# Position bias of the second block: factors of the product exchanged, results laid by query through DRAM

## The reference, cut to what matters

```python
bias = rel_bias[t5_bucket_2(pos_sel - pos_b[..., None])]   # 32 buckets, 16 heads
logits = jnp.einsum('bqhc,bqkc->bhqk', q_b, kv_sel) * scale
logits = logits + jnp.transpose(bias, (0, 3, 1, 2))
```

## Time and profile before

| | before |
|---|---|
| median of 3 runs | 1357.74 us (1356.25 to 1359.26) |
| profiled execution, its own time | 1356.31 us |
| span of that execution, first to last instruction | 1354.5 us |
| PE busy / PEld busy | 1335.7 us (99%) / 1194.7 us (88%) |
| DVE busy | 937.5 us (69%) |
| ACT busy | 419.5 us (31%) |
| POOL busy | 171.9 us (13%) |
| mean granted TensorE clock | 0.999 |

### The profile page before, as it was taken

The page is one execution under the profiler, slowest core; times in us unless marked ns, Lnnn a source line. Parts: engine busy times, 40 slices in busy tenths (PEclk is TensorE's granted clock), DMA queues, the critical chain, the costliest instruction groups (busy, mean ns, idle before and its releaser), DMA issues.

```text
span 1354.5 us, 21285 instructions
## 1 busy us (share of the span) xinstructions
PE 1335.7 (99%) x8873; PEld 1194.7 (88%) x8873; DVE 937.5 (69%) x1492; ACT 419.5 (31%) x892; POOL 171.9 (13%) x147
## 2 busy tenths in 40 slices
PE   9999999999999999999999999999999999999997
PEld 7976899988898599988888788889999995999986
DVE  4885798657598488867662778776887854856653
ACT  2154333220226333322056304435742103100101
POOL 3300322030200033114020000003100100011100
PEclk9999999999999999999999999999999999999999
DMA  9532567576432257756623251217644544545440
GB/s 321 187 124 94 187 222 276 213 274 215 169 126 93 94 208 281 258 210 225 216 63 105 85 184 63 79 62 255 209 144 142 217 161 151 162 151 187 171 171 31
DMA packets 127808, 229.76 MB, mean 170 GB/s; under 512 B 7094, under 2 KB 33998, under 8 KB 127458
## 3 DMA queue, kind: packets, MB, share of 16 engines
q1 hardware_dynamic: 123354, 218.26, 46.9%
q0 software_dynamic: 3952, 9.95, 2.2%
q10 hardware_dynamic: 407, 0.20, 0.1%
HBM read 227.30 MB, written 2.15 MB: 169 GB/s over the span
## 4 chain that ended last, share of the span: by engine, by line
PE 87%; DVE 7%; DMA 3%; issue 1%; ACT 1%; SPq 0%; DVEq 0%
PE acc L2033 55%; PE scr L2033 16%; PE pvw L2033 9%; DVE mid L1457 2%; DMA ring<-in_w_up 1%; PE scr L2132 1%; PE ptb L2141 1%; DMA ring<-in_w_in 1%; PE pvw L2631 1%; PE scr L2624 1%; DMA hid<-in_x 1%; DVE ring L1279 1%; PE scr L2602 1%; PE ptb L2033 1%; DVE ring L1219 1%
## 5 line engine op out<-in xcount | busy, mean ns | idle before, releaser
L2033 PE MATMUL acc<-y,ring 128*128 128x128 f32 (+2 forms) x1216 | 206.3, 325 | 1.1 <-ACT y L919 1.1
L2033 PEld LDWEIGHTS acc<-y,ring 128*128 128x128 f32 (+1 forms) x1216 | 182.9, 191 | 18.8 <-issue 2.9
L2033 PE MATMUL acc<-x,ring 128*128 128x128 f32 (+1 forms) x832 | 120.7, 299 | 0.0
L2033 PEld LDWEIGHTS acc<-x,ring 128*128 128x128 f32 x832 | 110.9, 192 | 5.8 <-issue 1.0
L2033 PE MATMUL acc<-ring,big 128*128 128x256 f32 (+1 forms) x376 | 115.5, 453 | 0.0
L2033 PEld LDWEIGHTS acc<-ring,big 128*128 128x128 f32 x376 | 70.6, 190 | 33.3 <-issue 26.9
L2033 PE MATMUL acc<-ring,hid 128*128 128x256 f32 (+1 forms) x364 | 98.8, 417 | 0.0
L860 ACT ACTIVATE ring<-ring,silc 128x512 f32<-128x512 f32 x96 | 60.1, 709 | 92.0 <-DMA ring<-in_ada_w 92.0
L2033 PEld LDWEIGHTS acc<-ring,hid 128*128 128x128 f32 x364 | 68.4, 190 | 21.7 <-issue 14.3
L2033 PE MATMUL acc<-ysq,ring 128*128 128x128 f32 x592 | 71.9, 275 | 0.1
L2033 PEld LDWEIGHTS acc<-ysq,ring 128*128 128x128 f32 x592 | 68.9, 192 | 0.4 <-ACT ysq L1008 0.4
(11 more groups left out here) (540 smaller groups left out, 2710.2 us busy)
## 6 DMA issues: line engine op xcount, KB each, us to landing
ring<-in_w_in SPq DMA_DIRECT2D x24, 2048.0 KB, 9.0
ring<-in_w_up SPq DMA_DIRECT2D x16, 2048.0 KB, 8.6
ring<-in_w_down SPq DMA_DIRECT2D x16, 2048.0 KB, 7.9
ring<-in_ada_w SPq DMA_DIRECT2D x12, 2048.0 KB, 12.9
ring<-in_w_ffn_in SPq DMA_DIRECT2D x22, 1024.0 KB, 6.7
ring<-in_w_out SPq DMA_DIRECT2D x6, 2048.0 KB, 8.1
ring<-in_w_o_ssd SPq DMA_DIRECT2D x4, 2048.0 KB, 8.1
ring<-in_w_ffn_out SPq DMA_DIRECT2D x4, 2048.0 KB, 7.6
```

Source lines behind the costliest of these rows:

```text
L2033: ins = pe.matmul(dst, w, m, start=start, stop=stop, is_transpose=turned, skip_group_check=True)
```

## The change

PE's two operands change places: the 64 columns of `blk` are now stationary, and 256 columns of the steps move. A matmul gives 64 rows (group and head) x 256 columns, and there are four for one bank: they go in turn to the lower and upper 64 partitions, two to each half of the bank (`bias_part`). A bank is one of 16 halves of chunks (`bias_made`), with group and head on the partitions and 4 positions x 256 on the free side. So that queries are what is spread over the chunks and keys are the 256 columns, the threshold's sign and the comparison are turned (`thr` is position plus `lo`, and `is_ge`). ACT and DVE copy a bank as it stands, 128 x 512.

`bias_made` lies in `hid` as `bias2` does. When both banks of a chunk are drained, POOL writes them to DRAM in two DMAs of 64 x 4 x 256 floats (256 KB; 16 such DMAs, 4.2 MB). When all have landed, four DMAs of 64 x 4096 floats (1 MB each) read them back into `bias2`, queries on the partitions. DVE waits for these four ahead of `logits2` at `b2 == FIRST2`.

```diff
--- before.py
+++ after.py
@@ -273,6 +273,7 @@
         isc, iwork = big[:, 12:14, :], big[:, 14:16, :]
         relu2 = work[:, 0:8, :].rearrange("p (a b) t -> p a b t", a=4)
         bias2 = hid[:, :, :].rearrange("p (t h) s -> p t h s", t=TT)
+        bias_made = hid[:, :, :].rearrange("p (n j) s -> p n j s", j=2)
         xtok2 = hid[:, 0:16, :].rearrange("p a b -> p (a b)").rearrange("p (t d) -> p t d", t=TT)
         ys = hid[:, 16:32, :]
         q2, qi2 = mid[:, 0:16, :], mid[:, 16:24, :]
@@ -305,6 +306,7 @@
         blank = upad[:, :, :].rearrange("p a b -> p (a b)")
         strips = nc.dram_tensor("strips", (4 * P * 2 * T + T,), F32).ap()
         acum_store = nc.dram_tensor("acum_store", (SSD_HEADS, T), F32).ap()
+        bias_store = nc.dram_tensor("bias_store", (64, 4 * HEADS2, T), F32).ap()
         gain_store = nc.dram_tensor("gain_store", (2, D), F32).ap()
         strip_rows = nc.dram_tensor("strip_rows", (4, 2 * T), F32).ap()
 
@@ -584,6 +586,16 @@
                 for c in range(DC):
                     pool.dma_start(gain_store[w:w + 1, c * P:(c + 1) * P].rearrange("o p -> p o"), mcol[:, 2 + w, c:c + 1]).then_inc(gains_out, 16)
 
+            for ci in range(8):
+                pool.wait_ge(drained, HEAD_ACCS + ACCS + DEPTH * LAYER_ACCS + BIAS_END[ci])
+                for i in range(2):
+                    pool.dma_start(bias_store[8 * ci + i:8 * ci + 8:2].rearrange("s p k -> p s k"),
+                                   hid[64 * i:64 * i + 64, 4 * ci:4 * ci + 4, :]).then_inc(bias_out, 16)
+            pool.wait_ge(bias_out, 16 * (5 + 16))
+            for g in range(4):
+                half = slice(64 * (g % 2), 64 * (g % 2) + 64)
+                pool.dma_start(bias2[half, g // 2, :, :], bias_store[:, HEADS2 * g:HEADS2 * g + HEADS2, :]).then_inc(bias_in, 16)
+
             def acum_row_pair(g, u):
 
                 if g >= 2:
@@ -907,10 +919,8 @@
 
             def bias_back(ci):
 
-                dst = bias2.rearrange("p t h (g s) -> p t s g h", g=4)
-                for t in range(TT):
-                    b = full()
-                    copied(dst[:, t, 8 * ci:8 * ci + 8], b[:, :, :].rearrange("p a b -> p (a b)").rearrange("p (s g h) -> p s g h", s=8, g=4))
+                for half in range(2):
+                    copied(bias_made[:, 2 * ci + half], full()[:, :, :])
 
             def modulated(first, gain, shift):
 
@@ -1333,7 +1343,7 @@
                 steps.mark(dve.tensor_copy(posqf[:, :], posq))
                 steps.mark(dve.tensor_copy(thr[:, :], posk[:, :]))
                 steps.sync()
-                steps.mark(ts(thr[:, :], thr[:, :], lo[:, 0:1], None, ALU.subtract))
+                steps.mark(ts(thr[:, :], thr[:, :], lo[:, 0:1], None, ALU.add))
                 steps.mark(ts(posq, posq, 6, None, ALU.arith_shift_right))
                 steps.mark(ts(post[:, :], post[:, :], 6, None, ALU.arith_shift_right))
                 steps.sync()
@@ -1392,7 +1402,7 @@
 
                     dve.wait_ge(filled, HEAD_ACCS + DEPTH * LAYER_ACCS + BIAS_END[ci - EARLY_BIAS])
                 tt(steps_of[ci % 3], over(posqf[:, :], 8), thr[:, 8 * ci:8 * ci + 8].unsqueeze(2).broadcast_to([P, 8, T]),
-                   ALU.is_le).then_inc(step_ready, 1)
+                   ALU.is_ge).then_inc(step_ready, 1)
 
             def head_combine(i, dst):
 
@@ -1412,8 +1422,7 @@
             def first_bias_back(t):
 
                 dve.wait_ge(filled, HEAD_ACCS + DEPTH * LAYER_ACCS + t + 1)
-                dve.tensor_copy(bias2.rearrange("p t h (g s) -> p t s g h", g=4)[:, t, 0:8],
-                                acc[t][:, :, :].rearrange("p a b -> p (a b)").rearrange("p (s g h) -> p s g h", s=8, g=4)).then_inc(drained, 1)
+                dve.tensor_copy(bias_made[:, t], acc[t][:, :, :]).then_inc(drained, 1)
 
             for l in range(DEPTH):
                 done = l * LAYER_ACCS + HEAD_ACCS + ACCS
@@ -1655,6 +1664,8 @@
                     conv2(b2 - 1)
                 if b2 in (0, 1):
                     select(b2)
+                if b2 == FIRST2:
+                    dve.wait_ge(bias_in, 16 * (8 + 4))
                 if b2 >= FIRST2:
                     for i in range(2):
                         k = 2 * (b2 - FIRST2) + i
@@ -2524,19 +2535,18 @@
                     ins = mm(ms, ones[:, which, :], src[:, c, :], c == 0, c == chunks - 1)
                 ins.then_inc(ms_full, 1)
 
-            def bias_part(b, ci, t, parts):
-
-                flat = b[:, :, :].rearrange("p a b -> p (a b)")
-                for s in parts:
-                    ins = mm(flat[:, 64 * s:64 * s + 64], steps_of[ci % 3][:, s, t * P:(t + 1) * P],
-                             blk[:, :, :].rearrange("p a b -> p (a b)"), True, True)
+            def bias_part(b, ci, half):
+
+                for s in range(4):
+                    ins = mm(b[64 * (s % 2):64 * (s % 2) + 64, s // 2, :], blk[:, :, :].rearrange("p a b -> p (a b)"),
+                             steps_of[ci % 3][:, 4 * half + s, :], True, True)
                 return ins
 
             def bias_products(ci, tiles=range(TT)):
 
                 pe.wait_ge(step_ready, ci + 1)
                 for t in tiles:
-                    bias_part(free_bank(), ci, t, range(8)).then_inc(filled, 1)
+                    bias_part(free_bank(), ci, t).then_inc(filled, 1)
 
             def turn(t, h, flat):
```

## The result

The changed kernel takes 1346.53 us (median of 5 runs, 1345.9 to 1348.08), the one before 1357.67 (5 runs): ratio 0.9924, 95% interval 0.9913 to 0.9935, that is 8.8 to 11.8 us less. The profiled execution took 1347.19 us, 9.12 less than that of before (1356.31); its span is 1345.2 us in place of 1354.5.

A forecast was written before the change was run, and what follows sets the result against it. TensorE, busy 99% of the span, was taken as the bound; 8.6 us from the second stretch plus 0.35 from the first, about 9.0, led to 1348.3 us, chance 0.70, range 1346.0 to 1352.2 (own range 1346.7 to 1350.2).

The forecast's parts named there:

- Where the gain lies: Bias products on TensorE: saving in the later gapless run moves everything behind it; earlier saving ends waiting for VectorE and ScalarE.
- second stretch: 160 bias records without a gap, 712.14 to 730.06 us; forecast 9.3 us in place of 17.9, 8.6 us less.
- B: Length of the second stretch, up to the transposes of `kvn`; forecast 8.6 us shorter.
- A: Length from the first bias product to the first product of the second stretch; forecast 0.35 us shorter.
- The price of a product: TensorE bias matmul, 64 stationary and 256 moving columns: taken as 0.116 us, one half's matmul running beside the other's.
- The other bound: TensorE bias matmul without overlap of the two halves: 0.223 us a record.
- Rival 1: Bias products' halves do not overlap: 0.223 us each, only 0.35 us gained, 1357 us, no change; chance 0.08.
- VectorE and ScalarE keep up: Compares and bank copies in the second stretch make TensorE wait for nothing: cost 0, with 0.3 us kept for copies.
- Rival 3: ScalarE's bank copies still cost 1.0 us and come late, some 2.3 us in all: 1350.6 us; chance 0.11.
- The first stretch: 96 bias records around the transposes from 683.91: 0.35 us gained by VectorE's shorter copy and ScalarE's earlier transposes, bounds 0 and 0.5.
- DRAM: Bias written out and read back by POOL, 8.4 MB: cost 0, reads ending about 785, 14 us before the logits.
- rival 2: Granted clock falls around the first stretch as TensorE idles: 3.6 us more, 1352 us; chance 0.07.

The follow-up runs named there:

- e2: Changed kernel with all bias products written to the lower 64 partitions, none to the upper; median 1355.78 us, ratio 1.0000 to the kernel before.
- e4: Changed kernel with ScalarE's 14 bank copies into a strided destination, as before the change; median 1347.49 us, ratio 0.9934 to the kernel before.
- e1: Changed kernel with products of three early banks done twice, 24 more records where TensorE waited; median 1346.40 us, ratio 0.9931 to the kernel before.
- e5: Kernel before the change with the changed kernel's plain bank copies on ScalarE and VectorE, products as they were; median 1355.39 us, ratio 0.9996.
- e9: Changed kernel with only VectorE's two copies of chunk 0 strided as before the change; one run, 1347.13 us.
- e8: Changed kernel with the four DRAM reads held on POOL until VectorE's convolution of the fifth double tile; median 1363.09 us, ratio 1.0051 to the kernel before.
- e7: Changed kernel with a fourth step buffer, chunk 3 compared and multiplied earlier, ahead of the gapless bias products; median 1344.91 us, ratio 0.9918 to the kernel before.
- e10: Changed kernel as it is, run again for a second look at the granted clock; one run, 1348.43 us.
- e3: Changed kernel with a chunk's eight matmuls four to the lower, then four to the upper partitions, except chunk 1; median 1348.89 us, ratio 0.9950 to the kernel before.

## Why the prediction was right

- **Where the gain lies.** Right: the second stretch moves the rest of the program, the first ends in a wait. B gave 9.12 us (forecast 8.6), A 0.58 (forecast 0.35), together 9.70, of which 9.36 show from the mark to the end. The sum was 8.95, the ratio's interval holds it. That the profiled executions as a whole also differ by 9.12 is chance.
- **The price of a product.** Right by the form that the trace already had the earlier trace rows: 0.116 taken, 0.119 by busy time, and 0.110 as 8.80 / 80, which is what B's extra 0.5 us come from. The other bound, 0.223, was measured in e2 (0.224). Rival 1 was priced rightly and is excluded.
- **VectorE and ScalarE keep up.** Right, with less room than counted for the compares: 0.12 us at chunk 7 where I had 0.5, as the products came sooner; and 0.18 us for the copies, where I had counted none at worst. Rival 3 is real if the stride is kept: 1.4 us in e4, where I had 2.3. Its price took the length of a lone strided copy, 1.04, for the pace of several in a row, which is 0.9.
- **The first stretch.** The size was too small and its reason half right. I had 0.35 us with an upper bound of 0.5; it is 0.67 where the clock holds (e1) and 0.58 in the profile of the changed kernel. I priced it by VectorE's copy and named the earlier transposes for ScalarE's part alone. The copy alone brings nothing (e5); the earlier transposes are 0.41 of 0.67 us, and the copy the rest (e9).
- **DRAM.** Right, and with 44 us to spare where I counted 14: the writes were done by 729.15 and not 743, the reads by 754.9 and not 785. That each us of lateness costs about one was shown by e8.
- **The clock.** Here the step failed that gave rival 2 a chance of 0.07. The argument was that the gaps are shorter than the 4 us at the end of the program; the clock fell with gaps of at most 2.13 us, in four of the six profiles with the changed first stretch. What was wrong on the other side is the price: 3.6 us were forecast, 0.1 to 1.4 came, because the low level lay mostly beside waits. That the result is the forecast's in spite of it is in part luck. By the Trainium skill ("TensorE: Matmul & The Clock Gate", Part 1) an idle array falls back to the lower level; here it fell though short runs of matmuls came between the waits, of which the longest was 2.13 us.
- The predicted 1348.3 lies 1.8 us above the median. The start was not the error: I had 1357.3, the median was 1357.67. The medians differ by 11.1 us and my sum by 9.0, while one execution against one, from the mark, gives 9.36. Of the five runs before, three took over 1357.6 us, of the five after one took over 1348; in three profiles (e5, e7, e10) everything is 1 to 3 us later after the fall of the clock at 82 to 88 us. That the longer of the other runs have the same cause is likely and not shown.

## What to carry to other kernels

If one factor of a product has 64 columns, make it the stationary one and send the results in turn to the two partition halves: a pair then costs what one costs, in full only in turn (e3), not at all in one half (e2). Then see whether the engines that feed and empty the banks keep the new pace: here they did by 0.1 to 0.2 us, and strided copies would have cost 1.4 (e4). Look first whether the trace already has a stream of that form, and take its price. Before counting the saving, ask what the stretch waits for: nothing of the time taken out ahead of a wait is gained, and it is room for work from a stretch that does bound the program (e7). When several DMAs must all have landed, take the slowest and not the median. And compare profiles from a mark ahead of the change: here that took a scatter of 2.9 us out, and differences of 0.1 us could be read.

## What was not expected of the hardware

- The granted clock fell to half in the middle of the program, in the changed kernel behind waits of 0.89, 0.88, 0.39 and 2.13 us with short runs of matmuls between them; in e4, with the same waits, it held.
- It fell also within 82 to 88 us, behind a wait of 2.0 to 2.1 us, in three of twelve profiles (e5, e7, e10), one of them a form of the kernel before; with the wait of e5, 2.06 us, it held in the kernel before itself.
- Four reads of 1 MB from DRAM on POOL's queue, issued within 2 us, landed 8.0 to 24.2 us after their issue in the changed kernel; the last landed 25.7 us after the first was issued, and 24.1 us at another place (e8).
- A ScalarE copy of a bank into a strided destination takes 1.03 to 1.18 us from its start to its end, but in a row one starts every 0.9 us (eight in 7.35, e4); a lone plain one takes 0.60, and five in a row 2.60.
